# A transformer block and two hybrid layers on one core: earlier block inversion, two value units convolved inside the first chunk, seven leading gate units, and reordered feeds

## The reference, cut to what matters

```python
def second_block(x, ...):
    for l in range(2):
        h = rms_norm(x, norm_w[l])
        x = x + hybrid_mixer(h, ...)
    return rms_norm(x, final_norm_w)

def hybrid_mixer(h, ...):
    qkv, z_a, a_lg, b_lg, cf_val, cf_glu, z_b, gate_lg = split(h @ w_in)
    qkv = silu(depthwise_conv_centred(qkv, qkv_conv_w))     # 5 taps, 1536 channels
    q, k, v = ...                                           # 4 heads of 128
    q, k = l2_normalize(q), l2_normalize(k)
    g = -exp(a_log) * softplus(a_lg + dt_bias); beta = sigmoid(b_lg)
    o = delta_rule(q, k, v, g, beta) + the same, backwards in time
    y_a = (norm(o) * dn_norm_w * silu(z_a)) @ w_dn_out
    u = depthwise_conv_centred(cf_val * sigmoid(cf_glu), cf_conv_w) + cf_conv_b  # 31 taps
    y_b = (silu(layer_norm(u)) * silu(z_b)) @ w_cf_out
    gate = sigmoid(gate_lg + gate_b)
    return (gate[0] * y_a + gate[1] * y_b) @ w_out
```

## Time and profile before

| | |
|---|---|
| median of three runs | 2199.97 us |
| profiled execution | 2199.35 us, its span 2198.1 us |
| TensorE busy | 2073.3 us, 94% of the span |
| VectorE, ScalarE, GpSimd busy | 1257.6, 884.1, 888.3 us |
| mean granted clock of TensorE | 0.984 of full speed |
| in the chain that ended last | TensorE 78%, VectorE 15%, ScalarE 5% |

### The profile page before, as it was taken

The page is one execution under the profiler, slowest core; times in us unless marked ns, Lnnn a source line. Parts: engine busy times, 40 slices in busy tenths (PEclk is TensorE's granted clock), DMA queues, the critical chain, the costliest instruction groups (busy, mean ns, idle before and its releaser), DMA issues.

```text
span 2198.1 us, 26552 instructions
## 1 busy us (share of the span) xinstructions
PE 2073.3 (94%) x10668; PEld 1653.8 (75%) x10668; DVE 1257.6 (57%) x1943; ACT 884.1 (40%) x1412; POOL 888.3 (40%) x431
## 2 busy tenths in 40 slices
PE   7999999999999999999999899799999999799997
PEld 5888787776666788888787687678778787678775
DVE  5422223746677533222225978898753779898653
ACT  4222233323444543222234376244544385353632
POOL 4444443332113344444343553444335553343342
PEclk9999999998999999999999999999999999999998
DMA  4343232321011232333232222101222222010232
GB/s 151 110 134 96 89 99 81 125 68 39 30 30 49 77 96 95 97 96 96 86 96 78 76 87 68 35 25 30 87 87 86 87 86 67 30 30 30 79 94 77
DMA packets 46185, 169.08 MB, mean 77 GB/s; under 512 B 5232, under 2 KB 6000, under 8 KB 45808
## 3 DMA queue, kind: packets, MB, share of 16 engines
q1 hardware_dynamic: 45344, 165.60, 24.1%
q10 hardware_dynamic: 720, 1.79, 0.2%
HBM read 165.27 MB, written 2.10 MB: 76 GB/s over the span
## 4 chain that ended last, share of the span: by engine, by line
PE 78%; DVE 15%; ACT 5%; issue 1%; DMA 1%; POOL 0%; DVEq 0%; ACTq 0%
PE ps L383 22%; PE ps L385 21%; PE ps L384 21%; PE ps L410 2%; DVE blk_t L1856 1%; DVE outer L1854 1%; DVE cu L1754 1%; PE ps L576 1%; PE ps L592 1%; PE ps L561 1%; ACT dl L1366 1%; PE ps L896 1%; DVE dl L1963 1%; PE ps L907 1%; PE ps L906 1%
## 5 line engine op out<-in xcount | busy, mean ns | idle before, releaser
L2082 POOL TENSOR_TENSOR wlo<-raw,whi 128x1024 fp32r<-128x1024 f32 x300 | 733.9, 2452 | 925.0 <-ACT whi L945 924.6
L383 PE MATMUL ps<-xh,whi 128*128 128x512 f32 x1600 | 652.8, 408 | 28.0 <-POOL wlo L2082 15.8
L385 PE MATMUL ps<-xh,wlo 128*128 128x512 f32 x1600 | 627.9, 392 | 0.0
L384 PE MATMUL ps<-xl,whi 128*128 128x512 f32 x1600 | 627.5, 392 | 0.0
L383 PEld LDWEIGHTS ps<-xh,whi 128*128 128x128 f32 x1600 | 303.1, 189 | 114.5 <-issue 29.5
L945 ACT CAST whi<-raw 128x1024 fp32r<-128x1024 f32 x300 | 312.5, 1044 | 180.9 <-DMA raw<-in_stream 180.8
L385 PEld LDWEIGHTS ps<-xh,wlo 128*128 128x128 f32 x1600 | 302.7, 189 | 65.3
L384 PEld LDWEIGHTS ps<-xl,whi 128*128 128x128 f32 x1600 | 303.4, 190 | 63.7 <-issue 6.0
L1754 DVE SCALAR_TENSOR_TENSOR cu<-up,lcols,cu 128x512 f32<-128x512 f32 x180 | 181.9, 1062 | 0.1
L1480 DVE TENSOR_TENSOR ml<-mid,mh 128x512 fp32r<-128x512 f32 x42 | 60.6, 1446 | 166.5 <-ACT mh L1001 166.5
L2118 POOL TENSOR_TENSOR cu<-cu,prod 128x512 f32<-128x512 f32 x60 | 87.6, 1460 | 152.7 <-ACT prod L1171 151.6
(11 more groups left out here) (343 smaller groups left out, 3019.9 us busy)
## 6 DMA issues: line engine op xcount, KB each, us to landing
raw<-in_stream SPq DMA_DIRECT2D x300, 512.0 KB, 3.6
w1k<-in_w SPq DMA_DIRECT2D x1, 2048.0 KB, 8.3
w1v<-in_w SPq DMA_DIRECT2D x1, 2048.0 KB, 9.6
outT<-h SPq DMA_DIRECT2D x4, 512.0 KB, 2.7
h<-in_xT ACTq DMA_DIRECT2D x2, 512.0 KB, 7.4
h<-in_xT SPq DMA_DIRECT2D x2, 512.0 KB, 7.8
mats<-in_mats ACTq DMA_DIRECT2D x1, 448.0 KB, 10.4
msk<-in_masks SPq DMA_DIRECT2D x1, 258.0 KB, 3.9
```

The lines of the kernel that those rows point to most:

```text
L383: pe.matmul(out, wh, hi, start=first, stop=False)
L384: pe.matmul(out, wh, lo, start=False, stop=False)
L385: return pe.matmul(out, wl, hi, start=False, stop=last)
L2082: pool.tensor_tensor(m.wlo[:, slot, :], m.raw[:, slot, :], m.whi[:, slot, :].bitcast(F32), ALU.subtract).then_inc(s.wlo)
```

## The change

- **Begin.** VectorE clears a tile, and TensorE multiplies it 28 times before any data is there (`warm_up`). ScalarE does one small activation during the transfers, splits all eight rows and the first four units, and then squares. `very_first_units` issues all high by high products, then those with low weights, then those with low rows. `norm(0)` stands behind the next unit.
- **Feed forwards.** The first two middle rows are split before the last pair. The down units take the column blocks in the order 4 to 7, 0 to 3, and only block 0 of the first waits for VectorE to free the banks. The last down unit follows four blocks behind the one before it. On ScalarE the casts of the down weights are placed anew, those of the first ones behind row 2.
- **Layer entry.** ScalarE may cast unit 5 behind the second normed row.
- **Block inversion.** The keys are scaled at j = 6, the decays summed behind unit 7, the products of keys stand behind unit 8 in banks 5, 3, 2, together with the spread of the decays, and the fourth block behind unit 9. The taps of unit 9 stand inside `block_matrices`. Units 10 and 11 (values) are copied by ScalarE and convolved by VectorE in the first chunk (`LATE_TAPS`), where their silus stand on ScalarE too. Queries are scaled behind step 12, the decay exponents stand behind step 20.
- **Lead.** `LEAD_UNITS` is 7, and the first products stand behind three units. GpSimd writes the identities of the first chunk at j = 4.

```diff
@@ TensorE
-LEAD_UNITS = 6
+LATE_TAPS = {"decay": 2, "level1": 1, "join1": 4, "level2": 3}
+UNIT_Q, DECAY_EXP = 12, 20
+LEAD_UNITS = 7
-FIRST_PRODUCTS = 2
+FIRST_PRODUCTS = 3
+WARM = 28
+    def very_first_units(u, outs):
+        for k in range(KD):
+            pe.wait_ge(s.xh, k + 1)
+            for n in range(2):
+                if k == 0:
+                    pe.wait_ge(s.whi, u + n + 1)
+                pe.matmul(outs[n], m.whi[:, (u + n) % RING, k * P:(k + 1) * P], m.xh[:, k, :], start=k == 0, stop=False)
+        pe.wait_ge(s.wlo, u + 2)
...
+    def warm_up():
+        pe.wait_ge(s.eps, 1)
+        for n in range(WARM):
+            pe.matmul(ps[:, 7, 0:P], m.ups[:, 0, 0:P], m.ups[:, 0, 0:P], start=True, stop=True)
...
-            for d in range(KD):
+            for d in (4, 5, 6, 7, 0, 1, 2, 3):
+                if i == 0 and d == 0:
+                    pe.wait_ge(s.g_scaled, NF * f + NF)
+                    pe.wait_ge(s.u_scaled, NF * f + NF)
...
+        for step in range(KD + 4):
+            if step < KD:
+                ins = multiply(u, step, ps[:, step, :], *mid_parts(m, NF - 2), False, False)
...
+            d = step - 4
+            if d == 0:
+                pe.wait_ge(s.wlo, u + 2)
+                pe.wait_ge(s.ml, NF * f + NF)
+            if d >= 0:
+                ins = multiply(u + 1, d, ps[:, d, :], *mid_parts(m, NF - 1), False, True)
...
-            if j == 8:
+            if j == 7:
                 pe.wait_ge(s.gl, l + 1)
                 pe.wait_ge(s.l2, 8 * l + 4)
...
+            if j == 8:
+                pe.wait_ge(s.qconv, 12 * l + 8)
                 for t in range(3):
-                    ins = keys_by_keys(ps[:, 5 + t, :], t)
+                    ins = keys_by_keys(ps[:, (5, 3, 2)[t], :], t)
...
-            if j == 10:
+            if j == 9:
                 pe.wait_ge(s.kk_read, 2 * l + 1)
                 keys_by_keys(ps[:, 5, :], 3).then_inc(s.d_kk)
@@ ScalarE
+        for i in range(2, NF):
+            u = u0 + 2 * NF + i
+            if i < NF - 2:
+                middle(i)
+                weights_upto(u + AHEAD + (0 if i == NF - 3 else 1))
...
-                if k == 5:
+                if k in (1, 5):
                     weights_upto(u0 + 2 * c + AHEAD + 4)
+        def raw_values(j):
+            act.wait_ge(s.unit, u0 + L_QKV + j + 1)
+            act.copy(m.qkv[:, QKV_ORDER[j], :], ps[:, j % 4, :]).then_inc(s.qkv)
...
+                if i == 0:
+                    j = 9 + lv
+                    act.wait_ge(s.qconv, 12 * l + j + 1)
+                    act.activation(m.qkv[:, QKV_ORDER[j], :], m.acc[:, j % 2, :], ACT.Silu).then_inc(s.qkv)
@@ VectorE
         def conv(point):
+            if late:
+                for j, n in late[0:LATE_TAPS[point]]:
+                    qkv_tap(j, n)
+                del late[0:LATE_TAPS[point]]
+                return
```

More of the change, by code:

```diff
@@ L425, in ffn @@
         first_units(u0, [ps[:, 0, :], ps[:, 1, :]], 2 * f)
-        norm(2 * f)
+        if f:
+            norm(2 * f)
         for i in range(1, NF):
@@ L430, in ffn @@
             x_unit(u0 + 2 * i, ps[:, 2 * (i % 2), :])
+            if f == 0 and i == 1:
+                norm(0)
             if i >= 2:
@@ L1269, in layer @@
                 act.activation(m.dsm[:, 4], m.dsm[:, 4], ACT.Exp).then_inc(s.cum_s)
-            if n == FIRST_PRODUCTS:
+        act.wait_ge(s.d_kk, 8 * l + 2 * l + 2)
+        diagonal_blocks(3, 5).then_inc(s.kk_read)
+        qkv_silu(9)
+        raw_values(10)
+        raw_values(11)
+        for n in range(LEAD_UNITS):
+            weights_upto(u0 + L_GATE + n + AHEAD + 1)
+            if n == 0:
+                l2_roots(4, (0, 1, 2, 3))
+            if n == FIRST_PRODUCTS + 2:
                 decays(l, 0)
@@ L1381, in scalar_engine @@
         weights_upto(min(k + 1, AHEAD))
+    weights_upto(AHEAD + 2)
+    for k in range(KD):
         square(0, k)
@@ L1463, in ffn, with middle @@
         inverse(2 * f)
+        def middle(i):
+            hi, lo = mid_parts(m, i)
+            dve.wait_ge(s.mh, NF * f + i + 1)
+            dve.tensor_tensor(lo, m.mid[:, i, :], hi.bitcast(F32), ALU.subtract).then_inc(s.ml)
         for i in range(NF):
@@ L1863, in inverse_blocks, with qkv_tap @@
             then(dve.tensor_copy(m.blk_w[:, 16:32, :], m.blk_l[:, 16:32, :]))
-        for j in range(12):
-            if j == 7:
+        def qkv_tap(j, n):
+            acc, src = m.acc[:, j % 2, :], ps[:, j % 4, :]
+            if j >= 10:
+                src = m.qkv[:, QKV_ORDER[j], :]
+            if n == 0:
+                if j < 10:
+                    dve.wait_ge(s.unit, u0 + L_QKV + j + 1)
+                else:
+                    dve.wait_ge(s.qkv, 14 * l + j + 1)
+                if j >= 2:
+                    dve.wait_ge(s.qkv, 14 * l + j - 1)
+            k = (2, 0, 1, 3, 4)[n]
+            w = lcl(m, l, "qkv_w", QKV_TAPS * QKV_ORDER[j] + k)
+            first, last = max(0, QKV_PAD - k), min(S, S + QKV_PAD - k)
+            if n == 0:
+                tapped["qkv"] = step(dve.tensor_scalar(acc, src, w, None, ALU.mult))
+                return
+            settle(tapped["qkv"])
+            ins = dve.scalar_tensor_tensor(out=acc[:, first:last], in0=src[:, first + k - QKV_PAD:last + k - QKV_PAD],
+                                           scalar=w, in1=acc[:, first:last], op0=ALU.mult, op1=ALU.add)
+            if n < QKV_TAPS - 1:
+                tapped["qkv"] = step(ins)
+            else:
+                ins.then_inc(s.qconv)
@@ L2052, in vector_engine @@
         x_low(0, k)
-        if k:
-            add_square(0, k)
+    for k in range(1, KD):
+        add_square(0, k)
     dve.wait_ge(s.in_par, 32)
@@ L2118, in shared_tap, with chunk, identities @@
             pool.tensor_tensor(m.cu[:, 3, :], m.cu[:, 3, :], m.prod[:, k % 2, :], ALU.add).then_inc(s.shared)
+    def chunk(l, i):
+        return [(d, 8 * l + 2 * i + d, delta_buffers(m, d), i if d == 0 else NT - 1 - i) for d in range(2)]
+    def identities(l, i):
+        for d, at, b, t in chunk(l, i):
+            if i:
+                pool.wait_ge(s.d_vn, at - 1)
+            else:
+                pool.wait_ge(s.qkv, 14 * l + 1)
+            pool.tensor_copy(b.T, all_heads(mat(m, "ident"))).then_inc(s.d_t0)
     def delta(l):
@@ L2128, in delta @@
         for i in range(NT):
-            both = [(d, 8 * l + 2 * i + d, delta_buffers(m, d), i if d == 0 else NT - 1 - i) for d in range(2)]
-            for d, at, b, t in both:
-                if i:
-                    pool.wait_ge(s.d_vn, at - 1)
-                else:
-                    pool.wait_ge(s.qkv, 12 * l + 12)
-                    pool.wait_ge(s.l2, 8 * l + 8)
-                pool.tensor_copy(b.T, all_heads(mat(m, "ident"))).then_inc(s.d_t0)
+            both = chunk(l, i)
+            if i:
+                identities(l, i)
+            else:
+                pool.wait_ge(s.l2, 8 * l + 8)
             for d, at, b, t in both:
```

163 lines of the change are left out of this document (86 added, 77 removed).

## The result

The changed kernel takes 2189.67 us (2184.2 to 2191.99), the kernel before 2199.89 in the same runs: ratio 0.995, interval 0.9937 to 0.9963. It is about 10 us faster where 27.7 were forecast, and outside the range that ended at 2188. Its profiled execution took 2191.99 us, its span 2190.7 at a mean clock of 0.981.

The account below looks back on a forecast made before the run. TensorE issues matmuls nearly all the time, so only its idle gaps and lower-clock stretches could give time. Terms 1.7+8.4-1.3+1.9+4.0+10.6+11.0-6.0-2.6 = 27.7 us gave 2172.3 us against the median, range 2157 to 2188.

Parts of the forecast that it names:

- Begin, 1.7: Kernel's begin: products start 7.0 us sooner, but the chain from norm's sum to unit 4 binds; net gain 1.7 us.
- The middles: Both feed forwards, gate to down: the waits for split middle rows and freed banks go, gaining 8.4 us in sum.
- the second end: End of the second feed forward: the last unit's four-block distance removes a wait and its lost clock, gaining 1.9 us.
- the entry: Layer 1's entry: the cast of unit 5 moves ahead of two casts of normed rows, gaining 2.0 us.
- layer 2's entry: Second layer's entry: some of the remaining wait for GpSimd's split weights goes, gaining 2.0 us.
- The first end: End of the first feed forward: VectorE's chain ends 2.7 us later relative to TensorE, with lost clock; net -1.3 us.
- 10.6 and 11.0: Value units and block inversion, layers 1 and 2: waits and lost clock removed, less new waits; gains in us.
- 3.0 and 1.3 each: Losses per layer in us: 3.0 from extra taps in the first chunk, 1.3 at the end of the chunks.
- New waits 6.5: Projections, per layer: waits for decays' sum 2.3, unit 7's taps 1.6, diagonal blocks 2.0 and gate result 0.6 us.
- the 17.1: Layer 1: removed waits for the inversion 10.0, its clock 2.1, scaled queries 2.9 and a gate result 2.1 us.
- rival A: Projections eat the gain: close new waits cut the clock, elimination ends late; layers' terms fall 7 each, 2186, chance 0.17.
- Five or six splits fall into the inversion now as then: Block inversion: as many GpSimd splits of 2.4 us inside it as before, so its length is kept, less 1.2 us.

Follow-up runs that it names:

- first_end_pairs: Changed kernel with the first feed forward's last down unit issued block by block beside the unit before it, as before the change: 2188.16 us (0.9948).
- picks_sooner: Changed kernel with the picked rows made before unit 7's taps, their sums copied sooner and their products ahead of the products of keys: 2173.54 us (0.9888).
- queries_later: Changed kernel with picks, diagonal blocks, fourth head's scaling and exponents sooner, fourth product's copies before unit 8's silu, queries scaled after step 17: 2176.07 us.
- sooner_taps_queries: queries_later with the picked rows before unit 6's taps, cleared states behind unit 7's taps and late taps 4, 1, 3, 2: 2185.02 us (0.9930).

## Why the prediction was wrong

**Begin, 1.7.** The chain from the norm's sum to unit 4 took the 10.0 us forecast (29.08 to 39.12), and the wait is 3.5. But the sum started at 29.1, not 27.7, and the clock was at 1.2 GHz from 38.0 to 44.8: 3.4 us lost instead of 1.6. Behind it the changed kernel is 0.8 us late for the same unit. By itself the begin gives nothing measurable.

**Feed forwards.** The middles gave 3.4 and 6.3, by GpSimd's splits on either side, against 8.4 in sum, the second end and the entry 3.9 as forecast (1.9 and 2.0), layer 2's entry 1.9 (2.0). The first end was forecast at -1.3 and cost 1.9: 3.2 won, 2.4 lost as the norm's wait grew from 1.4 to 3.8 (forecast 4.1), and 2.8 lost in 6.8 us at 1.2 GHz, where 1.6 were charged. The mechanism, VectorE's chain ending some 2.7 us later against TensorE, is in the trace. That the distance causes it is argued from the rows; first_end_pairs met another delay and does not decide it. Between the first end and the second feed forward another 0.5 went. So at the second feed forward nothing of the first was left, 0.1 us.

**Projections and inversion, 10.6 and 11.0 less 3.0 and 1.3 each: the failed step.** Forecast 6.3 and 6.7, measured -1.9 and -1.5; these 16.4 us are most of the 20 that were missed. In layer 1, in the changed kernel's times with its lead of 10.28 at the entry added:

- New waits 6.5, measured 9.9 with their clock. The decays' sums waited 2.4 (forecast 2.3). The taps of unit 7 ended at 1317.7 exactly as worked out, but nobody waited for them, nor for the diagonal blocks. The wait was for the picked rows, 3.7: the prediction let them take 4.1 with what follows, they took 8.0, since GpSimd held them (5.0 of the 7.0 us of picks, by the 1.96 that they take free). And both waits were followed by 1.7 us of lost clock, for which it had charged nothing.
- The inversion was to start at 1340.8 and started at 1347.0. The wait for the exponential is 4.86 (forecast 4.9); the 6.2 are 3.9 of the picks and 2.2 of the product with the keys, 3.43 for 1.23.
- Its result was to be there at 1386.4, ahead of TensorE at 1387. It came at 1394.4, and TensorE, itself delayed to 1392.7, waited 1.7 and 1.0 for its two halves, with 1.7 of clock: 4.4 of the 17.1 were not removed. The 3.0 in the sum for 1387 stands on no row. The last copy and the two selections took 5.0 us beside GpSimd; at the 1.8 that they take free of it, the result would have come 3.2 sooner and these waits would not be there.
- The chunks lost 4.9, forecast 4.3, but not where it was forecast, so the close sum is luck. The lead falls from 7.9 to 3.0 in the first chunk alone (the second chunk's first wait for `rt` ends at 1433.6 before and at 1430.6 now), where 3.0 were forecast. The late taps ran at 0.75 us each as priced; the larger part of the loss is the wait of 1.8 for the values' silu and its clock of 1.7. At the end of the chunks nothing was lost where 1.3 were forecast: the 35 taps of the last run took 29.75 us, the 30 before 28.55.

So the mechanism was rival A's in one half (new waits, each with the clock, and a late elimination), at 8 us a layer where A took 7; its 2186 had 0.17. The single step that failed is that the collisions with GpSimd were carried over as an average. "Five or six splits fall into the inversion now as then" held (6 instructions over 1 us against 8), but the picks, the product with the keys, the copy and the selections were priced free of them, and each was hit. The rows above show it for the wait of 3.7 and for that of 1.7 and 1.0, and two runs bear it out: with the same instructions at 2.0 instead of 7.0 us (picks_sooner) and at 1.8 instead of 5.0 (queries_later) these waits are gone. sooner_taps_queries is the reverse case: the picks stand sooner still, meet a split again, and TensorE waits 4.4 for the taps behind them. How much of the gain is the collision and how much the new place was not separated.

## What to carry over

Price each instruction that another engine waits for with and without the collision it can meet, and look in the trace for what the colliding instruction is tied to: if it follows the waiting engine's own progress, the result is either ahead of it or late by all of it. In the changed kernel's projections and first chunks each wait of 1.8 to 3.7 us was followed by 3.4 us at 1.2 GHz, which costs up to 1.7 us more, so one gap removed can be worth two. Not every such wait does that: the kernel before has waits of 2.9 at 1353.9 and of 2.1 at 1370.8 with the clock at 1.00 behind them. When a chain is moved sooner, find the next thing it waits for first (here the roots of the queries) and move that place with it.
